# A streaming encoder trunk: matmul order inside the feed-forward units, and the place of VectorE's weight split in the differential layer

## The reference

```python
for i in range(DEPTH):                                  # 4 layers
    h = rmsnorm(x, norm_mix[i])
    proj = h @ w_in[...]                                # mixer input and xq
    mix_out = mixer(proj[..., :-X_WIDTH])               # kind i % 3
    cross = memory_cross_attention(proj[..., -X_WIDTH:], mem_n, w_mem_kv[i], ...)
    x = x + jnp.concatenate([mix_out, cross], axis=-1) @ w_out
    x = x + jnp.square(jax.nn.relu(rmsnorm(x, norm_ffn[i]) @ w_ff1[i])) @ w_ff2[i]

def differential_attention(...):                        # 8 heads, two maps of 64 each
    q, k = rmsnorm(q, q_norm), rmsnorm(k, k_norm)
    p = softmax(q @ k.T * scale + bias)                 # for both maps
    attn = p[:, :, 0] - lam * p[:, :, 1]
    return rmsnorm(attn @ v, sub_norm) * (1.0 - lambda_init)
```

## Time and profile before

| | |
|---|---|
| median of three runs | 1813.42 us |
| the profiled execution, its own time | 1814.15 us |
| its span (first to last instruction) | 1812.1 us |
| PE busy | 1793.5 us (99%) |
| DVE busy | 1159.2 us (64%) |
| ACT busy | 1000.4 us (55%) |
| POOL busy | 319.5 us (18%) |
| DMA, mean over the span | 169 GB/s, granted TensorE clock 1.00 |

### The profile page before, as it was taken

One profiled execution on the slowest core, in us unless ns is written; L12 is line 12 of the kernel. 1 busy time (PEld: TensorE's weight loads), 2 busy tenths in 40 slices (PEclk: granted clock), 3 DMA queues, 4 the chain that ended last, 5 costly groups with the idle time before them and its releaser, 6 DMA issues.

```text
span 1812.1 us, 25915 instructions
## 1 busy us (share of the span) xinstructions
PE 1793.5 (99%) x9614; PEld 1537.8 (85%) x9614; DVE 1159.2 (64%) x1467; ACT 1000.4 (55%) x1601; POOL 319.5 (18%) x615
## 2 busy tenths in 40 slices
PE   9999999999999999999999999999999999999999
PEld 8998988888887778888888888888899987888887
DVE  5787775665665665565666546656677886556565
ACT  6666755544455665544455545444566666545443
POOL 2533550000012221000001300000144345000000
PEclk9999999999999999999999999999999999999999
DMA  7554443565555433555655435655554444355564
GB/s 272 167 167 147 141 140 111 169 196 188 190 180 177 150 125 120 170 191 190 191 198 187 164 127 175 198 189 193 177 177 148 153 139 134 113 195 186 188 193 130
DMA packets 85273, 305.65 MB, mean 169 GB/s; under 512 B 9632, under 2 KB 11040, under 8 KB 85152
## 3 DMA queue, kind: packets, MB, share of 16 engines
q1 hardware_dynamic: 84576, 302.88, 50.9%
q10 hardware_dynamic: 576, 1.12, 0.2%
HBM read 302.91 MB, written 1.05 MB: 168 GB/s over the span
## 4 chain that ended last, share of the span: by engine, by line
PE 96%; ACT 2%; DVE 2%; issue 1%; DVEq 0%; ACTq 0%
PE ps L1159 18%; PE ps L1161 18%; PE ps L1160 18%; PE ps L1181 13%; PE ps L1183 7%; PE ps L1170 3%; PE ps L1172 3%; PE ps L1171 3%; PE ps L1267 2%; PE ps L1317 2%; PE ps L1337 2%; PE ps L1199 1%; PE ps L1209 1%; ACT w_hi_t L1362 0%; PE ps L1132 0%
## 5 line engine op out<-in xcount | busy, mean ns | idle before, releaser
L1592 DVE TENSOR_TENSOR w_lo_t<-raw,w_hi_t 128x1024 fp32r<-128x1024 f32 x570 | 704.7, 1245 | 465.2 <-ACT w_hi_t L1362 464.1
L1362 ACT ACTIVATE w_hi_t<-raw 128x1024 fp32r<-128x1024 f32 x570 | 598.1, 1060 | 405.9 <-PE ps L1161 152.4
L1181 PE MATMUL ps<-hT,w_hi_t 128*128 128x512 f32 x1024 | 362.0, 397 | 0.0
L1159 PE MATMUL ps<-w_hi_t,act_hi 128*128 128x512 f32 x832 | 329.6, 396 | 0.0
L1161 PE MATMUL ps<-w_hi_t,act_lo 128*128 128x512 f32 x832 | 324.6, 390 | 0.0
L1160 PE MATMUL ps<-w_lo_t,act_hi 128*128 128x512 f32 x832 | 324.1, 390 | 0.0
L1183 PE MATMUL ps<-hT,w_lo_t 128*128 128x256 f32 x1024 | 287.4, 281 | 0.0
L1181 PEld LDWEIGHTS ps<-hT,w_hi_t 128*128 128x128 f32 x1024 | 192.3, 188 | 46.5
L1183 PEld LDWEIGHTS ps<-hT,w_lo_t 128*128 128x128 f32 x1024 | 193.4, 189 | 1.1
L1161 PEld LDWEIGHTS ps<-w_hi_t,act_lo 128*128 128x128 f32 x832 | 156.1, 188 | 33.7
L1159 PEld LDWEIGHTS ps<-w_hi_t,act_hi 128*128 128x128 f32 x832 | 156.3, 188 | 32.0
(11 more groups left out here) (215 smaller groups left out, 2448.6 us busy)
## 6 DMA issues: line engine op xcount, KB each, us to landing
raw<-in_wstream SPq DMA_DIRECT2D x570, 512.0 KB, 3.4
mix<-in_mem SPq DMA_DIRECT2D x4, 256.0 KB, 5.4
x<-in_x SPq DMA_DIRECT2D x1, 1024.0 KB, 9.3
wsT<-in_sgu_wT ACTq DMA_DIRECT2D x1, 512.0 KB, 4.6
sgain<-in_sgu_gain ACTq DMA_DIRECT2D x1, 512.0 KB, 5.5
out<-x SPq DMA_DIRECT2D x1, 512.0 KB, 2.8
out<-x SPq DMA_DIRECT2D x2, 256.0 KB, 2.0
consts_sb<-in_consts SPq DMA_DIRECT2D x1, 384.0 KB, 10.1
```

What stands on the lines that cost most here:

```text
L1159: pe.matmul(o, ah, wh[:, n], start=first and c == 0, stop=False)
L1181: pe.matmul(o.rearrange("p (a b) -> p a b", a=2), wh[:, n], hT2[:, :, kt, :], start=first and c == 0, stop=False, skip_group_check=True)
L1362: act.activation(w_hi_t[:, u % RING, :], raw[:, u % RING, :], ACT.Copy).then_inc(w_hi, 1)
L1592: dve.tensor_tensor(w_lo_t[:, u % RING, :], raw[:, u % RING, :], w_hi_t[:, u % RING, :].bitcast(F32), ALU.subtract)\
```

## The change

In the wide form all 8 matmuls of 512 columns come first and then all 8 of 256 columns. In the differential layer DVE takes each low part one unit later in the list of steps: at the step of unit u it takes that of u + 2, and the low part of u + 3 stands behind unit u's side steps, at the step of unit u + 1. ACT's casts keep their places. `low_later` is 1 for the steps made between the start of the first unit of the differential layer and the end of its output projection, and 0 elsewhere.

```diff
@@ class Plan, step
         kw["kind"] = kind
         kw.setdefault("w", len(self.units))
+        kw["low_later"] = self.low_later
         self.steps.append(kw)
@@ diff
         self.shared = True
+
+        self.low_later = 1
         for half in range(2):
@@ diff, at its end
         self.out_projection(i, l, DIFF, mix[:2] + cross[:2] + mix[2:] + cross[2:])
         self.shared = False
+        self.low_later = 0
@@ block.tensor, form "wide"
                         for c in range(UK):
                             kt = s["at"][0][c]
                             for f in range(4):
                                 ...
                                 pe.matmul(o.rearrange("p (a b) -> p a b", a=2), wh[:, n], hT2[:, :, kt, :], start=first and c == 0, stop=False,
                                           skip_group_check=True)
+                        for c in range(UK):
+                            kt = s["at"][0][c]
+                            for f in range(4):
+                                o = ps[:, job.banks[f], :]
+                                n = slice(c * COLS + f * P, c * COLS + (f + 1) * P)
                                 mm = pe.matmul(o[:, 0:SEQ], wl[:, n], hT2[:, 0, kt, :], start=False, stop=last and c == UK - 1,
                                                skip_group_check=True)
@@ block.vector
-                lo_to(s["w"] + AHEAD if k == "mm" else s["w"] + AHEAD - 1)
+                lo_to(s["w"] + AHEAD - (k != "mm") - s["low_later"])
```

## The result

The changed kernel takes 1803.59 us (median, 1803.06 to 1804.73) against 1814.11 us for the kernel before on the same chips (1812.96 to 1815.11): 10.5 us less, a ratio of 0.9945 with a 95% interval of 0.9935 to 0.9955. The forecast was 1803.4, in a range of 1799.5 to 1809.5.

The account below looks back on a forecast made before the run. PE was taken as the bound, by its matmul pace in feed-forward stretches and its waits in the differential layer. Gains of 4.8 and 5.2 us, 10.0 together, took 1813.4 to 1803.4 us, range 1799.5 to 1809.5.

Parts of the forecast that it names:

- The bound: Whole kernel: PE busy 99% of the span, so only shortening PE's own stream or its waits changes the time.
- Part 1: Wide units: eight long then eight short matmuls instead of alternating pairs, 363.3 us down to 358.5, gain 4.8 us.
- the 0.027 us of a return: Wide units: each change from 256 back to 512 columns costs 0.027 us, 128 times, 3.5 us.
- the wide form's operands: Rival, wide units: 512-column matmuls of this form take 233 ns anywhere; grouping loses 1.7 us, 1809.9 in all; chance 0.07.
- the price of the alternation: Wide units: an alternating pair takes 353 ns against 227 + 120 = 347 apart, so alternating costs 6 ns a pair.
- The rule by column count alone: Rival, wide units: matmul time follows column count, order gains nothing, only the differential layer's 5.2 us count: 1808.2; chance 0.10.
- Part 2: Differential layer: low parts one unit later cut PE's DVE-ended waits from 7.1 us to 1.85, gain 5.2 us.
- All four stretches: Differential layer near 600, 642, 650 to 661 and 698 us: PE's DVE-ended waits go, except 1.85 us in the third.
- the prediction's best case: Low end of the range, 1799.5 us: gains of 8.3 us in the wide units and 5.6 in the differential layer.
- The slack: Differential layer, tightest at unit 167: its delayed low part ends near 543.1, 1.7 us before PE starts the unit.
- Slower by late low parts: Rival, differential layer: PE waits at unit starts for low parts behind d_score, 17.6 us at eight heads, 1826; chance 0.04.

Follow-up runs that it names:

- the low parts alone: Kernel before with only DVE's low parts one unit later in the differential layer, wide units alternating as before: 1808.74 us against 1813.75.
- the joined order: Changed kernel with every second wide unit taking its 256-column matmuls first, so short ones of neighbouring units join: 1803.24 us against 1813.68 for the kernel before.
- the later cast: Changed kernel with ACT's cast right ahead of a turn of mix taken behind it, three places: 1802.36 us; with every second wide unit turned round too, 1801.00.
- the wide part alone: Kernel before with only the new matmul order inside the wide units, DVE's order as before: 1809.43 us against 1813.75.
- groups of four: Kernel before with only the wide units changed, 512- and 256-column matmuls changing over after four of each: 1811.29 us against 1813.75.

## Why the prediction was right, point by point

- **The bound.** PE in both stretches; the shares didn't move, and all of the time came out of PE's starts and PE's waits.
- **Part 1, 4.8 us forecast, 4.3 measured alone, 4.4 in the two traces (4.1 without the slow run of layer 1).** 227 and 120 ns hold, and so do the 0.027 us of a return and the 2.75 us of nat behind a run. The sum left out that the first short matmul behind long ones is about 7 ns quicker (a row of eight takes 0.95 us, not 0.96). Whether the cost sits in the change of size or in the wide form's operands, which the trace before could only suggest by one kind of matmul, is now shown: eight of this form in a row take 227 ns each.
- **What part 1 had too general: the price of the alternation.** It took the 353 ns a pair of one run for all 128 units. The run of 8 is cut after its first unit by eight transposes, and behind them, in layers 0, 2 and 3, the alternating order ran in another rhythm. First the kernel before, then the changed one, over the same seven units of layer 0:

```profile
351.93 0.48 PE L1181 MATMUL ps<-hT,w_hi_t 128*128 128x512 f32 x1
...
352.36 0.40 PE L1181 MATMUL ps<-hT,w_hi_t 128*128 128x512 f32 x1
...
371.43 0.39 PE L1159 MATMUL ps<-w_hi_t,act_hi 128*128 128x512 f32 x1
```

```profile
351.31 2.08 PE L1186 MATMUL ps<-hT,w_hi_t 128*128 128x512 f32 x8
...
370.94 0.40 PE L1164 MATMUL ps<-w_hi_t,act_hi 128*128 128x512 f32 x1
```

  From 352.36 to 371.43 there are 55 pairs, 347 ns each: this is 227 + 120, so the alternation costs nothing there, and the run takes 19.50 us. In groups of eight it takes 19.63, 0.13 more. The change pays in the runs that start behind long matmuls (11.15 instead of 11.30 us) and loses a little in these. In layer 1 the same seven units took 19.86 us in the profile before and 19.50 in that of the low parts alone, so one order can fall into either rhythm; what decides it isn't shown. The forecast's 363.3 us before are 362.3 by the trace, mostly for this reason, and its 358.5 after are 358.0.
- **The rule by column count alone** would have given nothing for part 1. It falls by 4.3 us in time and by 11.30, 11.20, 11.15 and 11.13 us for the same 64 matmuls in four orders. The section of the Trainium skill that the prediction quotes ("TensorE: Matmul & The Clock Gate", "Back-to-back issue gap") states this rule for one matmul by itself; for a stream with weight loads it gives 131 ns at 512 columns. The runs here don't agree with that either: 227 ns.
- **Part 2, 5.2 us forecast.** All four stretches came out as forecast. At 600, 642 and 698 us the waits vanished. At 660 us I had 1.85 us stay on L1652, 0.16 of it unseen: the list shows 1.77, so 1.93 stays, and the cause, ACT's chain, is shown by moving one cast.
- **What part 2 missed.** The run with late low parts in all layers, whose clock stayed at 1.00, shows the differential layer at 221.47 us (first matmul to first matmul), 6.0 us shorter, not 5.2, and above the 5.6 that the prediction's best case took for this part without deriving it. The difference lies partly in a wait that the list gave as "issue": PE started unit 169 at 550.58, 0.6 us after the matmul before it, when `norm_mul` (from 549.07 on, in 1.41 us) released its PSUM banks:

```profile
549.99 0.39 PE L1161 MATMUL ps<-w_hi_t,hT 128*128 128x512 f32 x1
550.58 0.47 PE L1159 MATMUL ps<-w_hi_t,hT 128*128 128x512 f32 x1 [0.21 <-issue]
```

  Against the usual 0.23 us that is 0.4 us lost, and it isn't there in the changed kernel. The rest lies in the first matmuls behind a wait (the one at 550.58 is followed after 0.31 us, not 0.23).
- **What it gave back.** The profiled execution had only 4.5 of those 6.0 us, for the reason under the last heading.
- **The slack.** Forecast 1.7 us for unit 167: the trace after has three low parts in a row from 540.21 on, the first done 1.2 us later at 541.4, and PE starts the unit at 543.19, 1.8 us left. No unit of the layer has less. The timeline of DVE, and PE's start:

```profile
539.07 1.22 DVE L1651 TENSOR_REDUCE stats<-nt 128x16 f32<-128x1024 f32 x1 [1.54 <-ACT nt L1452]
540.21 3.50 DVE L1602 TENSOR_TENSOR w_lo_t<-raw,w_hi_t 128x1024 fp32r<-128x1024 f32 x3
...
543.19 0.39 PE L1164 MATMUL ps<-w_hi_t,hT 128*128 128x512 f32 x1
```

- **The rivals.** Slower by late low parts was the right mechanism to fear: it sets in one unit further on (4.5 us of waits on L1602), and in the state-space layers already at one unit.

## What to carry to other kernels

On an engine that works in order, work that is due later but must wait for another engine belongs behind the work whose inputs are there, as far as its own slack reaches; measure that slack at its tightest place, and move it only where the bounding engine waits. Idle time in front of an instruction says nothing about its worth. Where matmuls of two lengths follow each other back to back, read their distances from start to start before taking a cost by length alone, and read them in every run: here one order had two rhythms, and grouping gained in most runs and lost in a few.

## What the hardware showed that I had not expected

**Behind two short waits the clock fell to half, in some executions.** In the profile of the changed kernel PE waits 1.77 us, does eight transposes, waits 0.83 us and goes on to `x_score`. PE's timeline there, in the kernel before and after:

```profile
661.11 1.06 PE L1209 MATMUL ps<-consts_sb,nt 128*128 128x128 f32 x8 [1.20 <-DVE nt L1652]
663.00 1.96 PE L1317 MATMUL ps<-kT,qT 128*128 128x256 f32 x8 [0.83 <-ACT kT L1429]
```

```profile
655.47 1.06 PE L1219 MATMUL ps<-consts_sb,nt 128*128 128x128 f32 x8 [1.77 <-DVE nt L1662]
657.36 3.48 PE L1327 MATMUL ps<-kT,qT 128*128 128x256 f32 x8 [0.83 <-ACT kT L1439]
```

The same eight matmuls of `x_score` take 3.48 us instead of 1.96. The window of 5 us around them shows a mean granted clock of 0.70 (the column behind POOL), and the stretch inside it 0.50, where all else is at 1.00:

```profile
655.00:660.00 5.00, 3.70 (x14) 3.04 (x15) 2.51 (x6) 2.54 (x10) 0.91 (x5) 0.70 0.26 84
657.10:660.40 3.30, 3.04 (x7) 2.52 (x8) 0.48 (x1) 1.58 (x9) 1.18 (x6) 0.50 0.48 159
```

So the engine went from its upper level (2.4 GHz) to the lower (1.2 GHz) for 3.4 us, which cost 1.5 us and hid part of what the change had won. It doesn't follow each time, and it doesn't look to be the change's own. The profiled runs of the changed kernel, of the low parts alone and of the joined order have it. That of the low parts in all layers has the same wait of 1.8 us without it, and five other executions of the changed kernel show a mean clock of 1.000 against the profiled one's 0.999, with spans 0.7 to 1.5 us shorter. No profiled run with a wait of 1.2 us there (the kernel before) or 0.8 us (the two kernels with the later cast) has it. But a mean clock of 0.999, with a span 1.1 to 2.2 us longer than at 1.000, stands at five of 28 executions of the kernel before and three of eleven of the wide part alone, none of them profiled, at four of six of the low parts alone and three of five of the joined order; two of six with low parts later in all layers have 0.998 and 3 us. None of the 11 in groups of four, of the 8 with low parts two units later, and of the 10 with the later cast has it. So the two waits are where the clock fell in three profiles; that they are the cause, and that a shorter wait prevents it, isn't shown, and what decides between two executions of one kernel stays open.

**A return to long matmuls is paid by several of them.** The 0.02 to 0.03 us behind a run of short ones, and 0.06 behind an alternation of 353 ns a pair, are spread over the first four to ten long matmuls. Why the engine takes that long to settle isn't shown by these runs.
